# Hybrid decoder layer on one core: GpSimd's weight sums issued inside the rounds of the recurrence

## What is computed

```
h = rmsnorm(x, g_pre_mix)
q_in, ckv, k_rope, lru_x, lru_y, gate_mla, gate_lru = split(h @ w_in)
o_mla = mla_attention(q_in, ckv, k_rope, ...) @ w_o_mla
xc = causal_dwconv(lru_x, w_conv_lru, b_conv_lru)        # 4 taps
r, i = sigmoid(xc @ w_rg + b_rg), sigmoid(xc @ w_ig + b_ig)
a = exp(-8 r softplus(-lam)); u = sqrt(1 - a^2) * (i * xc)
hr = scan(h_t = a_t h_(t-1) + u_t)
o_lru = (hr * gelu(lru_y)) @ w_o_lru
merged = sigmoid(gate_mla) * o_mla + sigmoid(gate_lru) * o_lru
x = x + rmsnorm(merged @ w_out, g_post_mix)
```

## Time and profile before

| | |
|---|---|
| time, median of 3 runs | 1705.45 us (1705.16 to 1705.82) |
| time of the profiled execution | 1704.79 us |
| its span, first to last instruction | 1702.7 us |
| mean granted TensorE clock | 0.998 |
| PE busy | 1693.7 us, 99% of the span |
| DVE / ACT / POOL busy | 76% / 58% / 16% of the span |
| rounds of the recurrence, about | 418 to 615 us of the span |
| DMAs of GpSimd for `sums` | 124, between 263 and 396 us and between 657 and 970 us |

### The profile page before, as it was taken

The page is one execution under the profiler, slowest core; times in us unless marked ns, Lnnn a source line. Parts: engine busy times, 40 slices in busy tenths (PEclk is TensorE's granted clock), DMA queues, the critical chain, the costliest instruction groups (busy, mean ns, idle before and its releaser), DMA issues.

```text
span 1702.7 us, 24655 instructions
## 1 busy us (share of the span) xinstructions
PE 1693.7 (99%) x8887; PEld 1452.7 (85%) x8887; DVE 1293.0 (76%) x1638; ACT 979.9 (58%) x1238; POOL 266.3 (16%) x340
## 2 busy tenths in 40 slices
PE   9999999999999999999999999999999999999998
PEld 7888888888888888888888888888888888888887
DVE  7766675468788897676887687779877778977797
ACT  7656655454577766455557575556555555545554
POOL 0012212220254431101211101110001110001100
PEclk9999999999999999999999999999999999999999
DMA  9644459997555549799999856556765556765555
GB/s 345 204 132 149 151 189 294 320 270 217 165 184 182 185 163 326 205 346 281 271 326 283 220 198 197 184 183 216 245 200 178 181 194 213 235 202 190 197 184 206
DMA packets 230872, 375.06 MB, mean 220 GB/s; under 512 B 8720, under 2 KB 165008, under 8 KB 228752
## 3 DMA queue, kind: packets, MB, share of 16 engines
q1 hardware_dynamic: 210992, 326.66, 56.9%
q0 software_dynamic: 13888, 32.51, 9.5%
q10 hardware_dynamic: 5920, 14.94, 2.3%
HBM read 369.89 MB, written 36.70 MB: 239 GB/s over the span
## 4 chain that ended last, share of the span: by engine, by line
PE 97%; DVE 1%; ACT 1%; issue 1%; POOL 0%; DMA 0%; SPq 0%; DVEq 0%; ACTq 0%; POOLq 0%
PE ps L636 48%; PE ps L711 30%; PE ps L958 8%; PE ps L650 3%; PE ps L803 2%; PE ps L941 1%; PE ps L867 1%; PE ps L773 1%; ACT wsp L1628 0%; PE ps L743 0%; PE ps L896 0%; PE ps L872 0%; PE ps L1340 0%; DMA raw<-in_w_in 0%; PE ps L682 0%
## 5 line engine op out<-in xcount | busy, mean ns | idle before, releaser
L2009 DVE TENSOR_TENSOR wsp<-raw,wsp 128x2048 fp32r<-128x2048 f32 (+2 forms) x304 | 673.5, 2229 | 185.7 <-ACT wsp L1405 164.1
L1405 ACT ACTIVATE wsp<-raw 128x2048 fp32r<-128x2048 f32 (+2 forms) x274 | 501.9, 1843 | 128.8 <-PE ps L711 92.0
L636 PE MATMUL ps<-asp,wsp 128*128 128x512 f32 x3032 | 529.0, 336 | 0.0
L636 PEld LDWEIGHTS ps<-asp,wsp 128*128 128x128 f32 x3032 | 463.5, 188 | 62.7 <-DVE asp L2604 0.3
L711 PE MATMUL ps<-wsp,hsp 128*128 128x512 f32 x1536 | 354.0, 390 | 0.0
L711 PEld LDWEIGHTS ps<-wsp,hsp 128*128 128x128 f32 x1536 | 287.5, 188 | 59.7
L636 PE MATMUL ps<-hsp,wsp 128*128 128x512 f32 (+1 forms) x1744 | 314.1, 338 | 0.0
L636 PEld LDWEIGHTS ps<-hsp,wsp 128*128 128x128 f32 x1744 | 268.1, 188 | 36.7
L711 PE MATMUL ps<-wsp,asp 128*128 128x512 f32 x768 | 175.1, 389 | 0.0
L1416 ACT ACTIVATE cr<-ps 128x256 f32<-128x256 f32 x185 | 69.1, 379 | 178.8 <-PE ps L636 158.3
L711 PEld LDWEIGHTS ps<-wsp,asp 128*128 128x128 f32 x768 | 144.0, 188 | 29.8
(11 more groups left out here) (336 smaller groups left out, 1532.3 us busy)
## 6 DMA issues: line engine op xcount, KB each, us to landing
raw<-in_w_up SPq DMA_DIRECT2D x88, 1024.0 KB, 5.3
raw<-in_w_in SPq DMA_DIRECT2D x56, 1024.0 KB, 5.4
raw<-in_w_in SPq DMA_DIRECT2D x32, 768.0 KB, 4.4
raw<-in_w_down SPq DMA_DIRECT2D x24, 1024.0 KB, 5.3
sums<-in_w_down POOLq DMA_DIRECT2D x76, 256.0 KB, 7.4
raw<-in_w_o_mla SPq DMA_DIRECT2D x16, 1024.0 KB, 9.8
raw<-in_w_o_lru SPq DMA_DIRECT2D x16, 1024.0 KB, 6.5
raw<-sums SPq DMA_DIRECT2D x31, 512.0 KB, 4.2
```

The lines of the kernel that those rows point to most:

```text
L636: mm = pe.matmul(ps[:, bank, 0:w], lhs(part, k), x[:, 0:w], start=(f and part == 0), stop=(l and part == 1))
L1405: act.activation(wsp[:, p0 % SLOTS, 0, 0:n], raw[:, p0 % SLOTS, 0:n], ACT.Copy).then_inc(hi_done, 1)
L2009: dve.tensor_tensor(wsp[:, slot, 1, 0:n], raw[:, slot, 0:n], wsp[:, slot, 0, 0:n].bitcast(F32), ALU.subtract).then_inc(lo_done, 1)
```

## The change

Of the 31 entries, the first 11 stay where they are. Entries 11 to 24 (four for WO, all eight for the first DN group, the first two for the second DN group) are issued inside the rounds of the recurrence, two entries a round. Entries 25 to 30 stay behind the end of GL's second half, as two batches of three. The wait for the end of GL's first half goes.

In round i (i from 1 to 7) GpSimd now does, after `y_mult(i - 1)` and ahead of its part of the recurrence: wait until all DMAs issued so far have landed; issue the four adds of the two entries copied in round i - 1; issue the four copies of the next two entries (none in round 7). Round 0 issues only the first four copies. GpSimd's rounds are written out instead of looped. After round 7 it waits for the last adds to land, and then does `y_mult(7)`. `sums_ready` gives the count of entry 25 for all of entries 11 to 24.

```diff
--- before.py
+++ after.py
@@ -106,7 +106,8 @@
         continue
     DN_SUMS[_n] = len(SUMS)
     SUMS += [(1024 * DN_PLANS[_n][c][2], GROUPS[_n][0] + 2 * DN_PLANS[_n][c][1]) for c in DN_MADE[_n]]
-SUM_BATCHES = [(0, 3), (3, 6), (6, 8), (8, 11), (11, 13), (13, 15), (15, 18), (18, 21), (21, 23), (23, 26), (26, 29), (29, 31)]
+SUM_BATCHES = [(0, 3), (3, 6), (6, 8), (8, 11), (11, 25), (25, 28), (28, 31)]
+LRU_SUMS = range(11, 25)
 
 
 def gl_sum(h, c):
@@ -2933,26 +2934,37 @@
             with pool.Fori(1, HEADS // 2) as u:
                 attention(u)
 
-            sums_done = [0]
+            sums_issued = [0]
+
+            def sum_block(at, k, b):
+
+                c0, k0 = SUMS[at]
+                w = w_in if at < GL_SUMS else w_out if WO_SUMS <= at < WO_SUMS + len(WO_MADE) else w_dn
+                return w[:, k0 + k, c0 + b * 512:c0 + b * 512 + 512]
+
+            def sums_landed():
+                pool.wait_ge(sums_step, sums_issued[0])
+
+            def sums_copied(ats):
+
+                for at in ats:
+                    for e in range(2):
+                        pool.dma_start(sums[at][:, e * 512:e * 512 + 512], sum_block(at, 0, 0)).then_inc(sums_step, 16)
+                        sums_issued[0] += 16
+
+            def sums_added(ats):
+
+                sums_landed()
+                for at in ats:
+                    pool.dma_start(sums[at][:, 0:512], sum_block(at, 0, 1), accum_op=ALU.add).then_inc(sums_step, 16)
+                    pool.dma_start(sums[at][:, 512:1024], sum_block(at, 1, 0), accum_op=ALU.add).then_inc(sums_step, 16)
+                    sums_issued[0] += 32
 
             def weight_sums(first, last):
 
-                def block(at, k, b):
-                    c0, k0 = SUMS[at]
-                    w = w_in if at < GL_SUMS else w_out if WO_SUMS <= at < WO_SUMS + len(WO_MADE) else w_dn
-                    return w[:, k0 + k, c0 + b * 512:c0 + b * 512 + 512]
-
-                def step():
-                    sums_done[0] += 16 * 2 * (last - first)
-                    pool.wait_ge(sums_step, sums_done[0])
-                for at in range(first, last):
-                    for e in range(2):
-                        pool.dma_start(sums[at][:, e * 512:e * 512 + 512], block(at, 0, 0)).then_inc(sums_step, 16)
-                step()
-                for at in range(first, last):
-                    pool.dma_start(sums[at][:, 0:512], block(at, 0, 1), accum_op=ALU.add).then_inc(sums_step, 16)
-                    pool.dma_start(sums[at][:, 512:1024], block(at, 1, 0), accum_op=ALU.add).then_inc(sums_step, 16)
-                step()
+                sums_copied(range(first, last))
+                sums_added(range(first, last))
+                sums_landed()
             for batch in SUM_BATCHES[:4]:
                 weight_sums(*batch)
             n0 = own.n
@@ -2966,8 +2978,10 @@
 
             def lru(i):
                 own.n, own.off = n0, i * 6
-                if not isinstance(i, int) or i:
+                if i:
                     y_mult(i - 1)
+                    sums_added(LRU_SUMS[2 * i - 2:2 * i])
+                sums_copied(LRU_SUMS[2 * i:2 * i + 2])
                 for e in range(2):
 
                     pool.wait_ge(gates_act, i * 4 + 2 * e + 2)
@@ -2978,15 +2992,14 @@
                     own.link(pool.tensor_scalar(RC[e], RC[e], 2.0, -1.0, ALU.mult, ALU.add))
                     pool.tensor_tensor(SQT[e], SQT[e], IG[e], ALU.mult).then_inc(lru_a, 1)
                 assert own.n == n0 + 6
-            rounds(pool, PH_LRU, lru, first_apart=True)
+            for i in range(PH_LRU.trips):
+                lru(i)
+            sums_landed()
             y_mult(PH_LRU.trips - 1)
             own.n, own.off = n0 + 6 * PH_LRU.trips, 0
 
-            pool.wait_ge(gemm_step, PH_GL[0].g_end)
-            for batch in SUM_BATCHES[4:6]:
-                weight_sums(*batch)
             pool.wait_ge(gemm_step, PH_GL[1].g_end)
-            for batch in SUM_BATCHES[6:]:
+            for batch in SUM_BATCHES[5:]:
                 weight_sums(*batch)
 
             def form_sums(n, pair):
```

## The result

The changed kernel takes 1719.56 us (median of 5 runs, 1718.06 to 1720.36) against 1705.45 us (5 runs, 1704.67 to 1705.93). The ratio is 1.0081, 95% interval 1.0070 to 1.0093: 14.1 us slower, where 11.9 us were forecast.

The account below looks back on a forecast made before the run. TensorE was taken as the bound, busy 1693.7 of 1702.7 us. Its stops in rounds 3 to 6, 5.8 + 0.2 + 2.3 + 3.6 = 11.9 us, gave a median of 1717.4 us; range 1705 to 1727.

Parts of the forecast that it names:

- No gain to be had: After the recurrence PE is busy 50.00 of 50 us, so taking the sums away there gives nothing.
- The stops and their places: In the rounds GpSimd waits for all its DMAs to land at DMA 58, 67, 71, 76, 85, 95, 99.
- The lengths: GpSimd's DMA sections, first to last issue, in rounds 2 to 7: 10.2, 20.3, 12.7, 16.8, 18.1, 10.3 us.
- two adds and two copies as three adds: Round 3, at DMA 71: the wait with these DMAs under way, for which no row stands, taken as 10.0 us.
- Four adds and two copies as five adds: Round 6, at DMA 95: the wait with these DMAs under way, taken as 17.0 us.
- The room: GpSimd's idle gaps in a round leave 12.0 us for the DMA section; the room at TensorE is about 0.5 us.
- the other place: TensorE stopped at the pieces that follow the second scan, named beside the gates; no separate size given.
- The 2.0 us given back: A GpSimd chain 4 us late starts after DVE's low part and avoids 2.0 us of contention, in three rounds.
- Hidden: Rival: DMAs land faster in the rounds, sections stay under 12.5 us, not slower, 1705.5 us; chance 0.10.
- No such wait: Rival: stops hang on something else and don't occur in the rounds; sections 4.3 us, time 1705.5; chance 0.08.
- weight loads late: Rival: DMA share 1.05 makes loads the bound, seven rounds stretch 8.4 us, time near 1726; chance 0.07.
- Faster: Rival: relief after the rounds removes PE idle time, worth under 1 us; chance of over 0.2%: 0.02.

## Why the prediction was right, and where its sizes were off

- **No gain to be had.** Right. The DMAs that left the stretch after the recurrence gave nothing back: the rounds are longer by 14.2 us and the kernel by 14.1.
- **The stops and their places.** Right in all seven, shown by the trace and by the kernels with 3584, 1536 and 2048 bytes. The seat was called plausible; the scratch space is now shown, since it alone moves the stops and takes the loss away. The counter's unit for an add was slightly wrong (17 to 9, not 2 to 1); at 2048 bytes both units give the same seven stops, so this cost the forecast nothing.
- **The lengths.** Predicted sections for rounds 2 to 7: 10.2, 20.3, 12.7, 16.8, 18.1, 10.3; measured 11.5, 22.8, 13.2, 15.6, 16.3, 10.5 us. The term taken without a row, two adds and two copies as three adds (10.0), measured 528.93 - 517.30 = 11.6. Four adds and two copies as five adds (17.0) measured 606.31 - 591.04 = 15.3, four adds (14.7) 577.97 - 564.61 = 13.4.
- **The room.** The 12.0 us were right: in round 3 GpSimd's chain was late by 10.9 us, against 22.8 - 12.0 = 10.8. So were the 0.5 us at TensorE: in rounds 5 and 6 the second scan came 2.6 and 2.7 us later within its round than before and TensorE lost 2.15 and 2.16, so 0.4 to 0.5 us is right. In rounds 3, 5 and 6 the wait fell in the main on the piece ahead of the gates, named as the other place (7.63, 1.46 and 1.18 us, against 0.26 and 0.17 at the gates). Round 4 cost nothing with 13.2 us: the slowed matmuls after round 3's stop had put the gate products 7.2 us behind the end of `y_mult` where it is 6.0 us in the earlier trace rows, which gave the section 1.2 us more.
- **The 2.0 us given back** by a product that misses DVE's low part: in round 3 it took 0.73 us in place of 2.78, and the scan was late by 8.8 us with GpSimd late by 10.9; the same product took 0.74 us in rounds 5 and 6. Right, and so the sum without it, 17.9 us, is not the one.
- **The term that was missing** is TensorE's clock. After the long stop it ran at 1.2 GHz for part of a piece, 2.0 us. Without it round 3 would be 7.9 us; 5.8 were forecast. Here 2.0 of the 2.2 us between forecast and result have their place; that the other errors nearly cancel is luck (by rounds 3 to 6 the forecast was 5.8, 0.2, 2.3 and 3.6 us, and 9.9, 0, 2.15 and 2.16 were measured).
- **Rivals.** "Hidden" fell: DMA 65 to 70 took 21.7 us against the 11.3 that it needed. With a quarter of the bytes the same stops are hidden, so stops can be hidden, and the bytes decide it. The estimate of 2.6 us for 256 KB by the Trainium skill, "DMA: Bandwidth & Descriptors" (Anatomy of one DMA — SWDGE (gpsimd) path), does not hold here: one add under way held GpSimd for 490.69 - 482.93 = 7.8 us, beside weight traffic. "No such wait" and "weight loads late" fell to the trace and to the last two windows. "Faster" did not happen.

## What to carry to other kernels

Before moving DMAs of GpSimd into a stretch where its work is on the path, number them and look for idle time of GpSimd put down to "issue" where they are made now: such stops come at fixed counts, cost a full drain of what is under way, and move with the DMAs. The price of a DMA there is not its 0.5 us of issue but the chance that the count is full at it, times the landing time of everything before it. What helps is a larger scratch space, fewer or smaller DMAs in one go, or, at a point where all have landed, a small DMA on another semaphore. That all have landed is not enough: here it is so at the start of every round, and the counts go on.

## What the runs showed of the hardware that was not expected

- GpSimd's DMAs of 128 rows fill two counts, one by 9 for a copy and 17 for an accumulating DMA, one by 9 for each, each up to one less than the scratch space divided by 16 bytes; when either is full GpSimd waits until all its DMAs have landed. The numbers are fitted to scratch spaces of 2048 and 3584 bytes, and tested by the exact places of 18 stops named beforehand (10 at 1536 bytes, 8 with seven more copies on the same semaphore).
- DMAs that signal another semaphore set both counts back to zero (five kernels), and one of 64 KB a round brings the ratio to the kernel before from 1.0081 to 0.9993. What lies behind it is open: whether it is the change of semaphore as such, or that DMAs with another semaphore have a space of their own, was not tried.
- A matmul takes about twice as long for some 4 us after 7.6 us without work, at a granted clock of 0.50; after stops of 1.2 and 1.5 us the clock stayed at 1.00. The kernel with 1536 bytes took 5.81 us for 32 matmuls after a stop of 1.9 us, 7.99 us after one of 6.2 us, and 8.70 us after one of only 3.6 us:

```profile
484.93 5.81 PE L637 MATMUL ps<-hsp,wsp 128*128 128x512 f32 x32 [1.87 <-DVE wsp L2010]
...
516.01 7.99 PE L637 MATMUL ps<-hsp,wsp 128*128 128x512 f32 x32 [6.16 <-DVE wsp L2010]
...
623.78 8.70 PE L637 MATMUL ps<-hsp,wsp 128*128 128x512 f32 x32 [3.56 <-DVE wsp L2010]
```

After that last stop the granted clock was 0.50 from 624 to 630 us. So a stop of TensorE can cost 2 to 3 us more than its own length, and the longer stop was not the one that cost more.
